# GpSimd's low parts in four pieces, and first high parts ahead of a dense GEMM's last eviction

## What is computed

```python
def even_layer(x, mem, rel_table, norm_g, w_in, ...):
    h = rms_norm_2(x, norm_g) @ w_in
    gq, gk, gv, gb, ga, gg, dq, dk, dv, dg, mq, mg = split_cols(h, EV_SPLITS)
    y = jnp.concatenate([
        gdn_branch(gq, gk, gv, gb, ga, gg, conv_w, a_log, dt_bias, gdn_gain),
        diff_attention(dq, dk, dv, dg, rel_table, dq_gain, dk_gain, lam, subln, lambda_init),
        memory_attention(mq, mg, mem, mem_norm, mem_w_kv, mem_qn, mem_kn),
    ], axis=-1)
    return x + y @ w_out

def odd_layer(x, mem, positions, rel_table, norm_g, w_in, ...):
    h = rms_norm_2(x, norm_g) @ w_in
    ...
    y = jnp.concatenate([window_attention(...), mla_attention(...), memory_attention(...)], axis=-1)
    return x + y @ w_out
```

## Time and profile before

| | us |
|---|---|
| median of 3 runs | 2891.98 (2890.57 to 2892.45) |
| the profiled execution | 2893.64 |
| its span in the trace | 2891.8 |

### The profile page before, as it was taken

One profiled execution on the slowest core, in us unless ns is written; L12 is line 12 of the kernel. 1 busy time (PEld: TensorE's weight loads), 2 busy tenths in 40 slices (PEclk: granted clock), 3 DMA queues, 4 the chain that ended last, 5 costly groups with the idle time before them and its releaser, 6 DMA issues. The chain is left out here.

```text
span 2891.8 us, 39412 instructions
## 1 busy us (share of the span) xinstructions
PE 2561.8 (89%) x14786; PEld 1893.3 (65%) x14786; DVE 1440.4 (50%) x2585; ACT 1109.0 (38%) x1975; POOL 487.9 (17%) x389
## 2 busy tenths in 40 slices
PE   8999999999888889999969979676899879958889
PEld 7984556885544444469858768565777657745667
DVE  5653883665211112247755544656455445454545
ACT  5544122453221222245444334343444334433434
POOL 0001010020111100000240220545300230052340
PEclk9999999999999999999979999788999989979999
DMA  7754334553699999935420145222344414421334
GB/s 297 224 201 150 142 135 153 181 199 119 275 422 422 422 422 421 384 138 176 163 80 18 45 160 189 73 102 73 131 147 180 168 69 160 153 99 41 132 116 146
DMA packets 80323, 529.79 MB, mean 183 GB/s; under 512 B 9089, under 2 KB 13569, under 8 KB 18849
## 3 DMA queue, kind: packets, MB, share of 16 engines
q1 hardware_dynamic: 76128, 514.50, 47.1%
q0 software_dynamic: 3456, 11.02, 1.5%
q10 hardware_dynamic: 576, 2.10, 0.2%
HBM read 520.24 MB, written 7.34 MB: 182 GB/s over the span
## 5 line engine op out<-in xcount | busy, mean ns | idle before, releaser
L753 POOL TENSOR_TENSOR ring_low<-ring,fill_wh 128x512 fp32r<-128x512 f32 x256 | 361.3, 1439 | 1159.7 <-ACT fill_wh L748 1159.2
L415 DVE TENSOR_TENSOR split_wl<-ring,split_wh 128x512 fp32r<-128x512 f32 x480 | 335.4, 706 | 251.5 <-ACT split_wh L383 250.0
L383 ACT ACTIVATE split_wh<-ring 128x512 fp32r<-128x512 f32 x480 | 300.7, 631 | 321.0 <-PE ps L355 317.4
L2296 PE MATMUL ps<-ring,yT 128*64 128x256 f32 x2048 | 247.9, 387 | 52.4 <-DMA ring<-in_weights 48.2
L353 PE MATMUL ps<-split_wh,x_high_part 128*128 128x512 f32 x672 | 267.9, 399 | 2.9 <-DVE split_wl L415 2.9
L354 PE MATMUL ps<-split_wl,x_high_part 128*128 128x512 f32 x672 | 266.1, 396 | 0.0
L355 PE MATMUL ps<-split_wh,x_low_part 128*128 128x512 f32 x672 | 266.0, 396 | 0.0
L786 PE MATMUL ps<-fill_wh,x_high_part 128*128 128x512 f32 x384 | 174.4, 454 | 77.8 <-PEq L2588 19.0
L2296 PEld LDWEIGHTS ps<-ring,yT 128*64 128x64 f32 x2048 | 137.8, 137 | 155.4 <-DMA ring<-in_weights 91.0
L1163 PE MATMUL ps<-ring,xT 128*128 128x512 f32 x512 | 222.0, 592 | 2.8 <-PEq L498 1.7
L748 ACT ACTIVATE fill_wh<-ring 128x512 fp32r<-128x512 f32 x256 | 145.3, 623 | 113.9 <-PE ps L788 51.6
(11 more groups left out here) (657 smaller groups left out, 5010.5 us busy)
## 6 DMA issues: line engine op xcount, KB each, us to landing
ring<-in_weights SPq DMA_DIRECT2D x468, 1024.0 KB, 5.3
x_res<-in_x SPq DMA_DIRECT2D x1, 2048.0 KB, 7.5
yT<-in_mem SPq DMA_DIRECT2D x1, 2048.0 KB, 15.5
rel_skew<-lru_feat POOLq DMA_DIRECT2D x1, 2048.0 KB, 50.0
mem_features<-yT ACTq DMA_DIRECT2D x4, 512.0 KB, 6.8
s_wb<-in_s_bc POOLq DMA_DIRECT2D x4, 512.0 KB, 4.1
s_wc<-in_s_bc POOLq DMA_DIRECT2D x4, 512.0 KB, 4.2
gate_bias<-in_gate_bias POOLq DMA_DIRECT2D x8, 256.0 KB, 4.0
```

The source lines that it names most:

```text
L383: nc.scalar.activation(wh[:, c % deep, :], raw(unit, turn, c), ACT.Copy).then_inc(w_high.sem, 1)
L415: last = nc.vector.tensor_tensor(wl[:, c % deep, :], raw(unit, turn, c), wh[:, c % deep, :], ALU.subtract)
L753: k.nc.gpsimd.tensor_tensor(self.low(step), k.ring[:, self.slot(step), self.columns(step)], self.high(step), ALU.subtract)\
L2296: last = nc.tensor.matmul(k.ps[s * WIN:(s + 1) * WIN, p, 0:FF], window[:, p, kc, :], k.ring[:, slot, at:at + FF], start=kc == 0, stop=kc = ...
```

## The change

Two edits. In `gemm_tokens` ACT's `fill.highs(act, 0)` stands ahead of the last `finish` and no longer behind it. In `make_low` POOL's subtraction of 128x512 becomes four of 128x128 over the same columns; the wait for the high part stands ahead of the first, and the semaphore is raised by the fourth. What is computed stays the same.

```diff
                 each_block_late(act, blocks, upb, body)
-                finish((blocks - 1) // 2, (blocks - 1) % 2)
                 if fill:
                     fill.highs(act, 0)
+                finish((blocks - 1) // 2, (blocks - 1) % 2)
...
         pool.wait_ge(high.sem, high.at(n))
-        k.nc.gpsimd.tensor_tensor(self.low(step), k.ring[:, self.slot(step), self.columns(step)], self.high(step), ALU.subtract)\
-            .then_inc(low.sem, 1)
+        whole, raw, taken = self.low(step), k.ring[:, self.slot(step), self.columns(step)], self.high(step)
+        for at in range(0, BLK, P):
+            part = slice(at, at + P)
+            last = k.nc.gpsimd.tensor_tensor(whole[:, part], raw[:, part], taken[:, part], ALU.subtract)
+        last.then_inc(low.sem, 1)
```

## The result

The changed kernel takes **2899.6 us** (median of 19 runs, 2889.6 to 2904.3), the kernel before 2890.6 (19 runs, 2885.8 to 2894.7): a ratio of 1.0027, interval 1.0018 to 1.0036, so 0.3% slower by these runs. The forecast was 2861 with a range of 2828 to 2883; it was wrong in size and in sign. The 19 times fall into two groups, 2889.6 to 2895.0 and 2898.1 to 2904.3; the profiled execution, 2893.3 us, is of the first. Two later measurements of the same kernel gave 2892.9 and 2889.6 (8 runs each, ratios 1.0010 and 0.9998; on two other chips, 2888.2 to 2897.2), all in or near the first group. The middle of the first group is 2893.1, that of the second 2901.9: the change costs 2 to 3 us in one group and 11 in the other, and it never gives the 30 us less.

What follows compares the result with a forecast made beforehand. PE was taken as the bound, through its waits. From 2892.0 us: 21.3 less (order edit), 30.7 more (piece cost), 22 and 20 less (DVE relief), in sum 32.6 less: 2859.4, rounded to 2861; range 2828 to 2883.

Steps and rivals of the forecast that it cites:

- The four signs: PE's wait at `diff_in` 4.5 to 5 us, six chunks in 9.9, line 2932 pairs near 1.4, line 2822 wait under 1.5.
- signs of being wrong: A piece over 0.5 us, lines 2929 and 2932 near 1.3 us an operation, or new PE waits for POOL at 786/787.
- Step 1: At four GEMMs' ends, high parts ahead of the last eviction shorten PE's waits: 21.3 us less in sum.
- Step 2: A 128-column piece on POOL costs 0.41 us, four 1.64, so a chunk costs 0.42 us more.
- pieces are nearly free: POOL's row of 256 columns is the right guide to piece cost; time 2823 us, halfway 2841; chance 0.2.
- Step 3: Piece cost counts only where POOL ends a stage or burst PE awaits: 73 chunks by 0.42, 30.7 us more.
- Step 4: In the differential attention, DVE waits only for a piece's rest, shortening PE's waits and half clock: 22 us less.
- Step 5: DVE relieved in rotary step, convolution, line 641, latent attention, norms and recurrence: together 20 us less.
- Queued pieces go first: POOL's already queued pieces go ahead of DVE's operation, so no relief comes anywhere; time 2901 us; chance 0.08.
- DVE's relief is hidden: Half of DVE's relief in the differential attention and elsewhere turns out covered; time 2880 us; chance 0.14.
- POOL becomes the pace: In the differential attention POOL sets the pace if a piece costs 0.55 us; time 2900 us; chance 0.08.

## Why the prediction was wrong

The sums go by spans of the profiled executions: before 2891.8, order edit alone 2866.8, both edits 2891.5. The prediction had the pieces at -11.3 (30.7 of price less 42 of relief); they came at +24.7, a miss of 36.

The four signs that the prediction named came, 4.88 us at the GEMM of `diff_in`, 10.02 for six chunks, pairs at 1.13 and 0.4 at the turn. They stand at the places that were to gain, so they could not show what was lost elsewhere. Of its signs of being wrong one came, the new waits of PE for POOL, at the ends of blocks.

**Step 1, the order edit: right.** 21.3 foretold, 21.7 in the four GEMM stages, 18.8 to 20.6 in the time. The rest of the profile's 25 is in attention blocks that vary by 1 to 3 us between traces.

**Step 2, the price of a piece: right.** 24 pieces took 10.02 us, 0.418 each, for 0.41 foretold. All widths together give 0.28, 0.418, 0.68 and 1.22 us for 64, 128, 256 and 512 columns: some 0.15 us fixed and 2.1 ns a column. The Trainium skill's GPSIMD Engine Reference, section Performance versus the Vector engine, led to an estimate of 0.18 us for the fixed part; the measurement is a little below. The row of 256 columns in the earlier trace rows was no guide (0.57 there, 0.68 here), and the rival that pieces are nearly free fell with it.

**Step 3, where it counts: right in kind, 4 us too low.** The GEMM stages are 10.4 us longer with pieces than with the order edit alone, for 10.1; ten other blocks that POOL ends are 18.2 us longer, for the 14.3 that their 34 chunks make.

**Step 4, the relief in the differential attention: right in kind, mis-sized.** 22 foretold, 16.4 found (132.6 to 116.3 us). The term itself came in whole: the waits at the turn of the scores went from 20.9 to 0.4, pairs of operations to 1.1 us. The rest was lost to what is late next, which the step did not ask. That was POOL's last burst, 5.42 us at the block's end, which item 3 did not count although POOL was to become busier in just this block:

```profile
1958.01 0.77 PE L789 MATMUL ps<-fill_wh,x_high_part 128*128 128x512 f32 x1 [5.42 <-PEq L2766]
```

**Step 5, the relief elsewhere: the step that failed.** It had 20 us less. The blocks that it names, first the change against the order edit alone (one trace each), then the length of the block in all traces with whole chunks or with pieces of 128 and no drain there:

| block | change, us | length, us |
|---|---|---|
| convolution | +1.3 | 172.8 whole, 174.0 or more in pieces |
| recurrence | -2.7 | 199.5 to 202.4 whole, 198.4 to 201.1 in pieces |
| first memory attention | +4.4 | 51.4 to 54.1 whole, 58.1 to 58.6 in pieces |
| rotary step | -1.4 | 33.6 to 34.6 whole, 31.5 to 32.2 in pieces |
| latent attention | +1.8 | 67.9 to 69.9 whole, 64.7 to 72.2 in pieces |
| second memory attention | +5.4 | 52.3 to 53.8 whole, 58.2 to 59.7 in pieces |

That is 8.9 us more in sum. The price of the 15 uncovered chunks in them is 6.3 us, so 2.6 us more are left where the step had 20 less: a miss of 23 of the 36. Steps 3 and 4 add 4 and 6; the rest is in blocks that the prediction left out. The step's premise was that DVE waits for what is left of one piece, 0 to 0.41 us, wherever it meets POOL. That is so for most of its operations, but not for a few that wait for the rest of POOL's row. In the two memory attentions line 641, down for a gain of 4 us, was passed over for 8.2 us of waiting each, and the blocks grew by 9.8 us where steps 3 and 5 together had 0.6 less; that being passed over is a part of it is shown by the run with whole chunks there and by that with drains. The other 12 us of the step's miss are relief that did not come or that PE did not feel. In the convolution the relief is real (9.45 to 4.74 us), but PE's waits moved to the block's end, where POOL's burst is now last: 1.3 us longer instead of 2.1 shorter. The rotary step gave 1.4 of 5, and the first halves of the norms nothing, since POOL ends those blocks. What the recurrence and the latent attention show is within what they vary by between traces.

**The median.** In the one trace of the second group the convolution's first operation is passed over as well: 7.5 us, which no profile of the first group shows. 11 of the 19 times are in that group, so the median is too.

**The rivals.** "Queued pieces go first" had a chance of 0.08 and the time 2901, next to the 2899.6; its mechanism is a part of the cause, though not as it was put, for all operations: it holds for a few, each for the rest of its burst. That the number came so near is luck: the rival had no relief at all, and 16 us of relief came. The prediction argued against it that DVE gets in after each operation in the trace; that was true of the subtractions of 1.2 us, and the wrong step was to carry it to operations a third as long. The Trainium skill's page SBUF — State Buffer, section Who interferes with whom, has it that the order of issue decides who blocks. Here 20 pieces that began after DVE's addition went ahead of it, and most other operations of DVE got in after one piece; the rule does not tell the two apart, and the trace decides. "DVE's relief is hidden" holds in the convolution, but by itself it gave 2880. "POOL becomes the pace" holds at the ends of the convolution and of the differential and memory attentions, and wholly with 64 columns.

What stays open: by what rule DVE is let in. Length and gaps matter (DVE is never passed over by the subtractions of 256 or 512 columns, and never with a drain), and the same instruction at the same place can go either way. Whether a drain helps by the gap or by holding back the pieces that queue behind it, no run tells apart.

## What to carry to other kernels

Cutting an engine's long operations to relieve another pays where the relieved chain is what the bound engine waits for, and only there: the same pieces gained 18.5 us in one block and lost some 40 in the others (2851.5 against 2893). Choose the largest piece that does it. Two pieces beat eight clearly (2844.9 against 2865.5) and four by a little (2851.5) in that block, and four clearly where all chunks are cut (2857.1 against 2899.6), since each cut costs fixed time at every end that the cut engine sets, and short pieces in a row can lock the other out for long. Price a relief by what is late next in the same block, with the cut engine's own last burst first.

## What the runs showed of the hardware

VectorE can be passed over by a row of short GpSimd operations. Behind pieces of 128 columns each such case lasted until the row's last piece: 8.8 to 8.9 us for one addition of 128x512 with two operands in SBUF, in both memory attentions of all seven traces with pieces of 128 columns there and no drain; 1.6 to 3.3 us for a 128x4 operation; 15.2 to 15.3 us for one 128x256 operation in two of these seven traces and 0.3 us of waiting in the others. Behind pieces of 64 columns the 128x4 operation took 3.2 to 3.5 us and got in while the row went on. It is not bound to this subtraction. In the latent attention of the changed kernel, line 2911 waits behind GpSimd's operations of line 1863, which are 0.57 us apart:

```profile
2648.74 5.76 POOL L1863 TENSOR_TENSOR odm_features<-odm_features,cols_sb 128x256 f32<-128x256 f32 x10
```

```profile
2651.32 3.21 DVE L2911 TENSOR_SCALAR att_stat<-att_stat 128x2 f32<-128x2 f32 x1
```

Behind the subtractions 0.68 and 1.22 us apart no trace shows it. A drain of GpSimd behind each four pieces costs 0.2 us, and with it no VectorE operation was held up for more than 0.3 us by the pieces.
